# Three products of 256 columns made into one of 512 and one of 256, in a float32 expert layer split into high and low parts

## The chip, the core and the metric

The kernel runs on one core of a Trainium2 chip. The metric is the device time of one execution in microseconds, median of several runs. The engines are TensorE (PE: matrix products; PEld: its weight loads), VectorE (DVE), ScalarE (ACT), GpSimd (POOL) and SyncE (SP, which issues all transfers of weights). Each runs its own list of instructions in order; semaphores tie the lists together.

## The reference

Three blocks work on 256 tokens of 1024 features: two layers of mixer and expert feed-forward, then one attention and pooling block. The change touches only the expert layers, which take most of the time:

```python
def peer_ffn(x, norm_ffn, w_query, sub_keys, expert_down, expert_up):   # twice
    xn = rmsnorm(x, norm_ffn)
    q = (xn @ w_query).reshape(B, S, 8, 2, 128)       # w_query 1024 x 2048
    s = einsum('bthpd,hpnd->bthpn', q, sub_keys)      # 128 keys, two halves, 8 heads
    s1, i1 = top_k(s[..., 0, :], 16); s2, i2 = top_k(s[..., 1, :], 16)
    top_s, top_c = top_k(all sums s1 + s2, 16)
    idx = i1[top_c // 16] * 128 + i2[top_c % 16]
    g = softmax(top_s)
    act = gelu(einsum('btd,bthkd->bthk', xn, expert_down[idx]))
    return einsum('bthk,bthkd->btd', g * act, expert_up[idx])  # 16384 experts
```

## The kernel before

Instead of gathering experts, the kernel computes all 16384 for all tokens, and multiplies by a gate that is zero where an expert was not picked. Each float32 operand is split in two parts of the type fp32r: high (a copy) and low (the difference). A product is the sum of high·high, high·low and low·high: three matrix products (`three`, lines 170 to 173), each with a weight load of its own.

Weights stream in chunks of 128 x 1024 values (512 KB), in four slots. For each chunk SP loads `raw` (`load`), ACT writes the high part `WH` (`high`, L154) once PE has left the slot, DVE (`low_v`, L159) or POOL (`low_g`, L164) writes the low part `WL`, and PE uses both. `on_gpsimd` names the chunks whose low part POOL makes: all of the queries ("wq"), and "down" chunks 0 to 31.

An expert layer has, per layer, 16 chunks of queries, 128 of "down" and 128 of "up". The functions `peer_tensor`, `peer_scalar` and `peer_vector` write the order of PE, ACT and DVE by hand, one step of the loop per chunk c:

- Queries: chunks 2h and 2h+1 fill two PSUM banks with head h, 256 tokens wide. ACT copies them to `QT` (L991). PE multiplies by the keys (`key_scores`, L861) one chunk later, ACT copies the scores (L942), and DVE picks the best 16 (`top16`, L1031 to L1039).
- Selection: after the last head DVE runs `select_pairs` (L1057 to L1102), one chain of some 60 us. PE turns the picks (`turn_picked`, L870, which waits for the semaphore `picked`) behind down chunk 28, and DVE makes tables of them (`picked_tables`, L1115 to L1126).
- Down: the weights are the expert chunk (stationary), the tokens XH and XL move, 256 columns at a time; a chunk takes 8 k-steps of `three` = 24 products. Two chunks share a bank, and ACT applies gelu from the bank to the array `G` (L1014).
- Gates: from chunk 29 on (SPREAD), 8 tokens every 3 chunks (PACE), 32 groups: DVE writes one-hot tables (L1136, L1142, L1147), ACT scales rows (L952, 8 per group), PE multiplies them (`products`, L882, 16 small products) into one of two pairs of banks, and DVE folds the gates into what `G` holds so far (L1154), ACT copies them ahead for the experts still to come (L958). For tokens whose gates are already there, gelu stays in PSUM (L1016) and DVE multiplies (L1164).
- Up: `G` is split in parts (L974, L1169) and is the weight operand; the expert chunk moves, 512 columns at a time, 12 products per chunk.

Of the kernel before, what the change touches and what calls it, by code (L numbers as in the profile page):

```python
# [7 lines left out]
ALU = mybir.AluOpType  # L8
# [9 lines left out]
NW = 4  # L18
# [53 lines left out]
def build(nc, d, out):  # L72
    ctx = ExitStack()
    with ctx:
# [7 lines left out]
        XH = sb("XH", [128, 8, 256], F32R)  # L82
        XL = sb("XL", [128, 8, 256], F32R)
# [15 lines left out]
        sb("ONE_REST", [128, 2048])  # L99
        CST = sb("cst", [128, C_N0])  # L100
# [701 lines left out]
        keys_in, wq_up, key_mm, s_up = (sem(n) for n in ("keys_in", "queries_up", "key_products", "key_scores"))  # L802
        arg_up, arg_exp, tk_up, tk_T, it_up = (sem(n) for n in (
# [5 lines left out]
        SPREAD, PACE, GROUPS = 29, 3, 32  # L809

        def fold_chunk(s):
            return SPREAD + PACE * s + 4

        def open_tokens(c):
            return 8 * sum(fold_chunk(s) <= c for s in range(GROUPS))


        TAILS, HEADS = {-1: 0}, {-1: 0}
# [3 lines left out]
        N_TAIL, N_HEAD = TAILS[127], HEADS[127]  # L822
# [3 lines left out]
        def parts_g(p):  # L826
            if p % 3 == 0:
                return GH, GL_
            return [v[:, 2 * (p % 3):2 * (p % 3) + 2, :].rearrange("p e t -> p (e t)") for v in (XH, XL)]
# [5 lines left out]
        def gate_bank(s):  # L835
            return 4 + 2 * (s % 2)

        def gate_view(s):

            b = gate_bank(s)  # L840
            return PS[:, b:b + 2, :].rearrange("p a n -> p (a n)").rearrange("p (t i) -> p i t", t=8)
# [10 lines left out]
        def key_scores(t, l, h):  # L852
            if h == 0:
                t.wait_ge(keys_in, 16 * l + 16)
            t.wait_ge(wq_up, 16 * l + 2 * h + 2)
# [17 lines left out]
        def products(t, l, s):  # L873
            t.wait_ge(col_s, 32 * l + s + 1)
            t.wait_ge(row_0, 256 * l + 8 * s + 8)
            t.wait_ge(row_1, 32 * l + s + 1)
            if s >= 2:
                t.wait_ge(fold_a, 32 * l + s - 1)
            for j in range(8):
                g, tt = divmod(j, 2)  # L880
                for k in range(2):
                    m = t.matmul(PS[:, gate_bank(s) + j // 4, (j % 4) * 128:(j % 4) * 128 + 128],  # L882
                                 ONE[:, s % 2, 0, g, :, tt], ROWS[:, s % 2, 1 + k, g, :, tt], start=(k == 0), stop=(k == 1))
            m.then_inc(prod, 1)

        def peer_tensor(t, l):
            wq, down, up = bases(l)
            n = 2 * l + 1
            norm_tensor(t, n, XS)

            def q_bank(pair, j):
                if pair >= 2:
                    t.wait_ge(wq_up, 16 * l + 2 * pair - 3 + j)
            for c in range(16):
                pair, kh = divmod(c, 2)
                chunk_T(t, wq + c, [PS[:, 2 * (pair % 2) + j, 0:256] for j in range(2)], 0, kh, 8,
                        n if pair == 0 else None, lambda j: q_bank(pair, j))
                if c >= 2 and c % 2 == 0:
                    key_scores(t, l, c // 2 - 1)
            for c in range(128):  # L900
                wait_low(t, down + c)
                if c < 8 and c % 2 == 0:
                    t.wait_ge(wq_up, 16 * l + 13 + c // 2)
                if c % 2 == 0 and c >= 8:
                    if open_tokens(c - 7):
                        t.wait_ge(act_gated, N_HEAD * l + HEADS[c - 7])
                    else:
                        t.wait_ge(act_tail, N_TAIL * l + TAILS[c - 7])
                o = PS[:, (c // 2) % 4, (c % 2) * 256:(c % 2) * 256 + 256]
                for k in range(8):  # L910
                    m = three(t, o, [v[:, (down + c) % NW, k * 128:k * 128 + 128] for v in (WH, WL)],
                              [v[:, k, :] for v in (XH, XL)], k == 0, k == 7)
                m.then_inc(w_used, 1)
                if c == 0:
                    key_scores(t, l, 7)
                if c == SPREAD - 1:
                    turn_picked(t, l)
                s, r = divmod(c - SPREAD - 3, PACE)
                if r == 0 and 0 <= s < GROUPS:
                    products(t, l, s)  # L920
            for c in range(128):
                p, j = divmod(c, 2)
                i = up + c
                wait_low(t, i)
                if j == 0:
                    t.wait_ge(g_low, 64 * l + p + 1)
                    if c == 0:
                        t.wait_ge(fold_a, 32 * l + 32)
                gh, gl = parts_g(p)
# [24 lines left out]

        def fold_scalar(a, l, s, c):
            n = c - c % 2
            a.wait_ge(fold_v, 32 * l + s + 1)
            a.activation(G[:, n:128, 8 * s:8 * s + 8], gate_view(s)[:, n:128], ACT.Copy).then_inc(fold_a, 1)  # L958
# [17 lines left out]
        def peer_scalar(a, l):  # L976
# [4 lines left out]
            for c in range(16):  # L981
# [3 lines left out]
                if c % 2:  # L985
# [4 lines left out]
                    for j in range(2):  # L990
                        a.activation(QT[:, 2 * pair + j, :], PS[:, 2 * (pair % 2) + j, 0:256], ACT.Copy).then_inc(wq_up, 1)  # L991
            for c in range(128):
# [3 lines left out]
                if c == SPREAD - 14:  # L996
                    gate_exp(a, l)
                s, r = divmod(c - SPREAD - 1, PACE)
# [4 lines left out]
                s, r = divmod(c - SPREAD - 4, PACE)  # L1003
                if r == 0 and 0 <= s < GROUPS:
                    fold_scalar(a, l, s, c)
                if c == 127:
                    split_g_scalar(a, l, 0)
                if c % 2:
                    ps, g, k = pair_view((c // 2) % 4), G[:, c - 1:c + 1, :], open_tokens(c)
                    a.wait_ge(w_used, down + c + 1)  # L1010
                    if c == 77:
                        a.wait_ge(it_up, l + 1)
                    if k < 256:
                        a.activation(g[:, :, k:256], ps[:, :, k:256], ACT.Gelu_apprx_tanh).then_inc(act_tail, 1)  # L1014
                    if k:
                        a.activation(ps[:, :, 0:k], ps[:, :, 0:k], ACT.Gelu_apprx_tanh).then_inc(act_head, 1)  # L1016
# [23 lines left out]

        def select_keys(v, l):
            for h in range(8):
                v.wait_ge(s_up, 8 * l + h + 1)
# [105 lines left out]
        def fold_vector(v, l, s, c):  # L1149
            n = c - c % 2  # L1150
# [3 lines left out]
            v.tensor_tensor(g, gate_view(s)[:, 0:n], g, ALU.mult).then_inc(fold_v, 1)  # L1154

        def gate_vector(v, l, c):

            k = open_tokens(c)
# [5 lines left out]
            v.tensor_tensor(g, pair_view((c // 2) % 4)[:, :, 0:k], g, ALU.mult).then_inc(act_gated, 1)  # L1164
# [17 lines left out]
        def peer_vector(v, l):  # L1182
# [10 lines left out]
            for c in range(128):  # L1193
                low_v(v, down + c + 2)
                if c % 2 == 0 and c > 0:
                    gate_vector(v, l, c - 1)
                s, r = divmod(c - SPREAD, PACE)
                if 0 <= s < GROUPS:
                    (onehots, scale_columns, rows_part1)[r](v, l, s)
                s, r = divmod(c - SPREAD - 4, PACE)  # L1200
                if r == 0 and 0 <= s < GROUPS:
                    fold_vector(v, l, s, c)
                if c == 127:
                    split_g_vector(v, l, 0)
            gate_vector(v, l, 127)
# [1130 lines left out]
```

## Time and profile before

| | |
|---|---|
| median of 3 runs | 2197.97 us (2196.89 to 2198.56) |
| profiled execution | 2198.79 us; its span 2197.0 us, mean granted clock 0.994 |
| PE, PEld busy | 98%, 90% |
| DVE, ACT, POOL busy | 63%, 56%, 17% |
| HBM read | 369.96 MB, 169 GB/s over the span |

In the first layer queries run from 146 to 197 us, down from 197 to 598 us, up from 598 to 946 us; the second layer has the same stages, some 937 us later. Busy shares are of the whole span. A PE record of a product is longer than the distance to the next one, as products overlap, so what a product costs is read from start to start.

### The profile page before, as it was taken

What the parts mean: (1) busy time and instruction counts of PE and PEld (TensorE: products, weight loads), DVE (VectorE), ACT (ScalarE), POOL (GpSimd) and SP (SyncE); (2) the same over time, 40 slices, a digit from 0 to 9 for tenths busy, and PEclk for the clock granted to TensorE, in tenths of its full rate; (3) what the DMA queues carried; (4) which work ended last, traced back from release to release, by engine and by line L of the source; (5) the groups of instructions that cost most, each with busy time, mean ns of one, the idle gap of its engine ahead of it and who ended that gap; (6) DMA issues with size and microseconds to landing.
All of it is one profiled execution on the core that took longest, in us unless ns stands there. A gap on an engine that the chain in (4) does not pass through costs nothing.

```text
span 2197.0 us, 36208 instructions
## 1 busy us (share of the span) xinstructions
PE 2154.4 (98%) x14640; PEld 1968.7 (90%) x14640; DVE 1378.2 (63%) x2369; ACT 1235.9 (56%) x2086; POOL 370.3 (17%) x168
## 2 busy tenths in 40 slices
PE   8899999999999999997999999999999999999998
PEld 7789999999988888876899999999888888898997
DVE  7657867777755555557479567777555555423445
ACT  6654567777644444465555677776444444444463
POOL 1437810000000000001378100000000000243131
PEclk9999999999999999999999999999999999999999
DMA  6444554455566666642345545544666666754233
GB/s 217 145 135 164 184 172 164 163 164 167 162 200 192 195 196 191 192 161 94 125 161 186 173 160 168 167 162 163 201 192 192 192 194 194 250 188 145 84 130 115
DMA packets 104330, 373.41 MB, mean 170 GB/s; under 512 B 11565, under 2 KB 15045, under 8 KB 103781
## 3 DMA queue, kind: packets, MB, share of 16 engines
q1 hardware_dynamic: 104164, 371.11, 52.3%
q8 instruction: 116, 1.90, 0.3%
q14 instruction: 50, 0.40, 0.1%
HBM read 369.96 MB, written 1.10 MB: 169 GB/s over the span
## 4 chain that ended last, share of the span: by engine, by line
PE 92%; DVE 3%; ACT 2%; DMA 1%; issue 1%; POOL 0%; SPq 0%; ACTq 0%; DVEq 0%
PE ps L171 28%; PE ps L172 28%; PE ps L173 28%; PE ps L882 3%; PE ps L1862 1%; PE ps L1840 1%; DMA raw<-in_w_qk_dram 1%; DVE WL L159 1%; PE ps L267 1%; PE ps L861 1%; PE ps L1848 0%; DVE arena L1598 0%; PE ps L277 0%; PE ps L1322 0%; ACT WH L154 0%
## 5 line engine op out<-in xcount | busy, mean ns | idle before, releaser
L154 ACT ACTIVATE WH<-raw 128x1024 fp32r<-128x1024 f32 x680 | 717.5, 1057 | 541.4 <-PE ps L173 525.3
L171 PE MATMUL ps<-XH,WH 128*128 128x256 f32 x2816 | 807.3, 287 | 3.7 <-DVE XL L2146 2.8
L172 PE MATMUL ps<-XL,WH 128*128 128x256 f32 x2816 | 797.7, 283 | 0.0
L173 PE MATMUL ps<-XH,WL 128*128 128x256 f32 x2816 | 797.5, 283 | 0.0
L159 DVE TENSOR_TENSOR WL<-raw,WH 128x1024 fp32r<-128x1024 f32 x548 | 670.5, 1226 | 102.9 <-ACT WH L154 102.5
L171 PEld LDWEIGHTS ps<-XH,WH 128*128 128x128 f32 x2816 | 540.9, 192 | 9.4 <-DVE XL L2146 3.0
L172 PEld LDWEIGHTS ps<-XL,WH 128*128 128x128 f32 x2816 | 541.5, 192 | 0.1
L173 PEld LDWEIGHTS ps<-XH,WL 128*128 128x128 f32 x2816 | 541.0, 192 | 0.0
L164 POOL TENSOR_TENSOR WL<-raw,WH 128x1024 fp32r<-128x1024 f32 x132 | 328.6, 2494 | 1011.1 <-ACT WH L154 1010.2
L171 PE MATMUL ps<-WH,XH 128*128 128x512 f32 x960 | 379.1, 395 | 4.4 <-DVE XL L725 1.6
L172 PE MATMUL ps<-WL,XH 128*128 128x512 f32 x960 | 375.8, 391 | 0.0
L173 PE MATMUL ps<-WH,XL 128*128 128x512 f32 x960 | 375.7, 391 | 0.0
L171 PEld LDWEIGHTS ps<-WH,XH 128*128 128x128 f32 x960 | 181.6, 189 | 45.1 <-issue 2.0
L173 PEld LDWEIGHTS ps<-WH,XL 128*128 128x128 f32 x960 | 181.5, 189 | 38.3
L172 PEld LDWEIGHTS ps<-WL,XH 128*128 128x128 f32 x960 | 181.4, 189 | 37.5 <-issue 0.5
L952 ACT ACTIVATE ONE<-ONE,GATE 128x128 f16<-128x128 f16 x512 | 167.3, 428 | 0.0
L1169 DVE TENSOR_TENSOR XL<-arena,XH 128x512 fp32r<-128x512 f32 x84 | 58.1, 692 | 164.9 <-ACT XH L974 164.9
L1014 ACT ACTIVATE arena<-ps 128x512 f32<-128x512 f32 (+31 forms) x126 | 55.3, 439 | 147.6 <-PE ps L173 147.5
L171 PE MATMUL ps<-WH,GH 128*128 128x512 f32 x352 | 137.0, 389 | 0.0
L172 PE MATMUL ps<-WL,GH 128*128 128x512 f32 x352 | 137.0, 389 | 0.0
L173 PE MATMUL ps<-WH,GL 128*128 128x512 f32 x352 | 136.9, 389 | 0.0
L1758 POOL TENSOR_TENSOR arena<-arena,trig 128x128 f32<-128x128 f32 x8 | 4.2, 555 | 722.0 <-DVE arena L1598 722.0
(279 smaller groups left out, 1829.5 us busy)
## 6 DMA issues: line engine op xcount, KB each, us to landing
raw<-in_l_down_dram SPq DMA_DIRECT2D x256, 512.0 KB, 3.4
raw<-in_l_up_dram SPq DMA_DIRECT2D x256, 512.0 KB, 3.9
raw<-in_l_wq_dram SPq DMA_DIRECT2D x32, 512.0 KB, 3.4
raw<-in_w_qk_dram SPq DMA_DIRECT2D x24, 512.0 KB, 3.5
raw<-in_w_gates_dram SPq DMA_DIRECT2D x24, 512.0 KB, 3.5
raw<-in_l_nat_dram SPq DMA_DIRECT2D x16, 512.0 KB, 3.9
raw<-in_l_wout_dram SPq DMA_DIRECT2D x16, 512.0 KB, 3.5
raw<-in_l_win_dram SPq DMA_DIRECT2D x16, 512.0 KB, 4.1
```

Of the source, the lines that this page charges most:

```text
L154: a.activation(WH[:, i % NW, :], raw[:, i % NW, :], ACT.Copy).then_inc(w_high, 1)
L159: v.tensor_tensor(WL[:, i % NW, :], raw[:, i % NW, :], WH[:, i % NW, :], ALU.subtract).then_inc(w_low_v, 1)
L164: g.tensor_tensor(WL[:, i % NW, :], raw[:, i % NW, :], WH[:, i % NW, :], ALU.subtract).then_inc(w_low_g, 1)
L171: t.matmul(o, a[0], b[0], start=first, stop=False)
L172: t.matmul(o, a[0], b[1], start=False, stop=False)
L173: return t.matmul(o, a[1], b[0], start=False, stop=last)
L267: t.matmul(PS[:, bank, 384:512], ident, ident, start=True, stop=True)
L861: m = t.matmul(PS[:, 4 + h % 4, (2 * tt + q) * 128:(2 * tt + q) * 128 + 128], QT[:, j, tt * 128:tt * 128 + 128], KEYS[:, j * 128:j * 128 + ...
L882: m = t.matmul(PS[:, gate_bank(s) + j // 4, (j % 4) * 128:(j % 4) * 128 + 128], ONE[:, s % 2, 0, g, :, tt], ROWS[:, s % 2, 1 + k, g, :, tt ...
L952: a.activation(ROWS[:, s % 2, 1, g, :, t], ROWS[:, s % 2, 2, g, :, t], ACT.Copy, scale=GATE0[:, 8 * s + j:8 * s + j + 1]).then_inc(row_0, 1)
L1014: a.activation(g[:, :, k:256], ps[:, :, k:256], ACT.Gelu_apprx_tanh).then_inc(act_tail, 1)
L1169: v.tensor_tensor(gl, G[:, 2 * p:2 * p + 2, :].rearrange("p e t -> p (e t)"), gh, ALU.subtract).then_inc(g_low, 1)
```

## The change

- XH and XL lie side by side for each k in one tile X2 (128 x 8 x 2 x 256). `two` multiplies the high weights by both at once (512 columns, a whole bank), then the low weights by XH (256 columns, into the bank's lower half). It replaces `three` in the 16 query chunks and in down chunks 26 to 127 (WIDE = 26) of each layer. The halves of a bank have to be added afterwards.
- Queries: ACT copies the upper halves (128x512 for two banks, `queries_low`), DVE adds the lower ones (`queries`, new, 8 per layer); the add for head h+1 stands before `top16` of head h.
- Down from 26 on: each chunk has a bank of its own, six in turn (0 to 5). For each pair ACT copies the upper halves to BESIDE (`copy_beside`), DVE adds (`down_add`: tokens without gates into `G`, the others into PSUM), and ACT applies gelu one loop step later (`gelus`). `products` now has only banks 6 and 7.
- Gates are spread from chunk 25 on: `turn_picked` stands behind down chunk 24 and chunk 26 waits for the tables (`it_up`). `rows_part1` and the fold stand a chunk later against the group's first step, `gate_vector` and the copies of `fold_scalar` too.
- POOL makes the low parts of down chunks 0 to 27 only.

```diff
-        return name[3:] == "wq" or c < 32
+        return name[3:] == "wq" or c < 28
-        XH = sb("XH", [128, 8, 256], F32R)
-        XL = sb("XL", [128, 8, 256], F32R)
+        X2 = sb("X2", [128, 8, 2, 256], F32R)
+        XH, XL = X2[:, :, 0, :], X2[:, :, 1, :]
+        def two(t, bank, w, k, first, last):
+            t.matmul(PS[:, bank, :], w[0], X2[:, k, :, :].rearrange("p w t -> p (w t)"), start=first, stop=False)
+            return t.matmul(PS[:, bank, 0:256], w[1], X2[:, k, 0, :], start=False, stop=last)
...
-        SPREAD, PACE, GROUPS = 29, 3, 32
+        SPREAD, PACE, GROUPS = 25, 3, 32
+        WIDE = 26
-            return SPREAD + PACE * s + 4
+            return SPREAD + PACE * s + 5
+        def down_bank(c):
+            return (c - WIDE + 4) % 6 if c >= WIDE else (c // 2) % 4
...
# products
-            if s >= 2:
-                t.wait_ge(fold_a, 32 * l + s - 1)
+            if s >= 1:
+                t.wait_ge(fold_a, 32 * l + s)
# peer_tensor, down
+                before = bank_before(c) if c % 2 == 0 else None
+                if c == WIDE:
+                    t.wait_ge(it_up, l + 1)
+                elif before is not None:
...
+                    if c >= WIDE:
+                        m = two(t, b, w, k, k == 0, k == 7)
+                    else:
+                        m = three(...)
                 if c == SPREAD - 1:
                     turn_picked(t, l)
-                s, r = divmod(c - SPREAD - 3, PACE)
+                s, r = divmod(c - SPREAD - 4, PACE)
# ACT, new
+        def copy_beside(a, l, c):
+            n, b = pair_at(c), down_bank(c - 1)
+            a.wait_ge(w_used, bases(l)[1] + c + 1)
+            if c - 4 > WIDE:
+                a.wait_ge(added, N_ADD * l + ADDS[c - 4])
+            a.activation(BESIDE[:, n % 2], PS[:, b:b + 2, 256:512], ACT.Copy).then_inc(beside, 1)
# DVE, new
+        def queries(v, l, h):
+            q = QT[:, 2 * h:2 * h + 2, :]
+            v.wait_ge(wq_low, 8 * l + h + 1)
+            v.tensor_tensor(q, PS[:, 2 * (h % 2):2 * (h % 2) + 2, 0:256], q, ALU.add).then_inc(wq_up, 1)
+        def down_add(v, l, c):
+            k, n, b = open_tokens(c), pair_at(c), down_bank(c - 1)
+            v.wait_ge(beside, PAIRS * l + n + 1)
+            if k < 256:
+                v.tensor_tensor(G[:, c - 1:c + 1, k:256], PS[:, b:b + 2, k:256], BESIDE[:, n % 2, :, k:256],
+                                ALU.add).then_inc(added, 1)
+            if k:
+                o = PS[:, b:b + 2, 0:k]
+                v.tensor_tensor(o, o, BESIDE[:, n % 2, :, 0:k], ALU.add).then_inc(added, 1)
# peer_vector, down loop
-                if c % 2 == 0 and c > 0:
-                    gate_vector(v, l, c - 1)
+                if c % 2 == 0 and c > WIDE:
+                    down_add(v, l, c - 1)
                 s, r = divmod(c - SPREAD, PACE)
-                if 0 <= s < GROUPS:
-                    (onehots, scale_columns, rows_part1)[r](v, l, s)
+                if r == 0 and 1 <= s <= GROUPS:
+                    rows_part1(v, l, s - 1)
+                if r == 0 and 0 <= s < GROUPS:
+                    onehots(v, l, s)
+                if r == 1 and 0 <= s < GROUPS:
+                    scale_columns(v, l, s)
...
+                if c % 2 and c > WIDE + 1:
+                    gate_vector(v, l, c - 2)
```

PE behind down chunk 24, first the program before (there 24 is like any other chunk; its picks come behind 28), then the changed one at the turning of the picks. L171 to L173 are `three`, L870 is `turn_picked`:

```order
L173 MATMUL ps<-XH,WL 128x256
L171 MATMUL ps<-XH,WH 128x256
L172 MATMUL ps<-XL,WH 128x256
L173 MATMUL ps<-XH,WL 128x256
L870 MATMUL ps<-cst,arena 128x128 [waits key_scores,picked]
```

After the change L172 to L174 are `three`, L891 is `turn_picked`, and L178 and L179, from chunk 26 on, are `two`:

```order
L174 MATMUL ps<-X,WL 128x256
L891 MATMUL ps<-cst,arena 128x128 [waits key_scores,picked]
L891 MATMUL ps<-cst,arena 128x128 x5
L172 MATMUL ps<-X,WH 128x256 [waits w_low_g]
...
L178 MATMUL ps<-X,WH 128x512
L179 MATMUL ps<-X,WL 128x256
L178 MATMUL ps<-X,WH 128x512
L179 MATMUL ps<-X,WL 128x256
```

The picks are turned with one full chunk (25) between them and the first `two`.

DVE in the down stage, some three chunks of the program before, in the middle of the gates' spreading (L159 low part, L1164 gate, L1147 `rows_part1`, L1136 one-hots, L1142 scaling, L1154 fold):

```order
L159 TENSOR_TENSOR WL<-raw,WH 128x1024 [waits w_high]
L1164 TENSOR_TENSOR arena<-ps,arena 128x2x88 [waits gates_copied,gelu_open]
L1147 TENSOR_TENSOR ONE<-ONE,GP 128x1024 [waits rows_part0]
L159 TENSOR_TENSOR WL<-raw,WH 128x1024 [waits w_high]
L1136 TENSOR_TENSOR ONE<-IOT,IB 128x1024 [waits gate_products]
L1136 TENSOR_TENSOR ONE<-IOT,IB 128x1024
L159 TENSOR_TENSOR WL<-raw,WH 128x1024 [waits w_high]
L1164 TENSOR_TENSOR arena<-ps,arena 128x2x88 [waits gates_copied,gelu_open]
L1142 TENSOR_TENSOR ONE<-ONE,EB 128x1024 [waits onehots]
L1154 TENSOR_TENSOR arena<-ps,arena 128x66x8 [waits gelu_new,gate_products]
```

The same place after (L160 low part, L1229 and L1233 `down_add`, L1215 `rows_part1`, L1204 one-hots, L1210 scaling, L1243 gate, L1222 fold):

```order
L160 TENSOR_TENSOR WL<-raw,WH 128x1024 [waits w_high]
L1229 TENSOR_TENSOR arena<-ps,BESIDE 128x2x192 [waits down_beside]
L1233 TENSOR_TENSOR ps<-ps,BESIDE 128x2x64
L1215 TENSOR_TENSOR ONE<-ONE,GP 128x1024 [waits rows_part0]
L1204 TENSOR_TENSOR ONE<-IOT,IB 128x1024 [waits gate_products]
L1204 TENSOR_TENSOR ONE<-IOT,IB 128x1024
L160 TENSOR_TENSOR WL<-raw,WH 128x1024 [waits w_high]
L1210 TENSOR_TENSOR ONE<-ONE,EB 128x1024 [waits onehots]
L1243 TENSOR_TENSOR arena<-ps,arena 128x2x64 [waits gates_copied,gelu_open]
L160 TENSOR_TENSOR WL<-raw,WH 128x1024 [waits w_high]
L1229 TENSOR_TENSOR arena<-ps,BESIDE 128x2x184 [waits down_beside]
L1233 TENSOR_TENSOR ps<-ps,BESIDE 128x2x72
```

Two adds per pair of chunks are new, and `rows_part1` has moved to stand directly before the next group's one-hots.

## Rows read from the trace of the kernel before

**Rows 1.** Windows: selection, early and late gates, up (busy us; clock; DMA).

```profile
core 0: us, PE busy (x) PEld busy (x) DVE busy (x) ACT busy (x) POOL busy (x), PEclk, DMA share, GB/s
200.33:281.00 80.67, 80.67 (x675) 80.67 (x674) 66.18 (x182) 41.25 (x47) 68.04 (x29) 1.00 0.55 181
300.00:396.13 96.13, 96.13 (x882) 95.70 (x882) 66.70 (x95) 69.84 (x151) 0.00 (x0) 1.00 0.50 165
492.00:588.13 96.13, 96.13 (x883) 95.70 (x882) 76.69 (x95) 67.50 (x152) 0.00 (x0) 1.00 0.51 163
600.00:930.00 330.00, 330.00 (x1457) 273.26 (x1456) 186.63 (x184) 159.65 (x182) 0.00 (x0) 1.00 0.62 194
```

**Rows 2.** The page's chain that ended last, its line by engine.

```profile
PE 92%; DVE 3%; ACT 2%; DMA 1%; issue 1%; POOL 0%; SPq 0%; ACTq 0%; DVEq 0%
```

**Rows 3.** Timeline of PE, products of 256 columns: down chunks 1 to 28.

```profile
200.53 0.28 PE L172 MATMUL ps<-XL,WH 128*128 128x256 f32 x1
...
280.93 0.28 PE L173 MATMUL ps<-XH,WL 128*128 128x256 f32 x1
281.05 0.82 PE L870 MATMUL ps<-cst,arena 128*128 128x128 f32 x6
281.62 0.36 PE L171 MATMUL ps<-XH,WH 128*128 128x256 f32 x1
```

**Rows 4.** Timeline of PE, products of 512 columns at the end of up.

```profile
937.98 0.39 PE L171 MATMUL ps<-WH,XH 128*128 128x512 f32 x1
...
945.91 0.39 PE L173 MATMUL ps<-WH,GL 128*128 128x512 f32 x1
```

**Rows 5.** The critical chain, first and last gate products (start, us).

```profile
293.37 0.93 PE ps L882 x16
...
591.38 0.94 PE ps L882 x16
```

**Rows 6.** DVE timeline, late gates (start, us, idle before).

```profile
586.35 0.67 DVE L1164 TENSOR_TENSOR arena<-ps,arena 128x496 f32<-128x496 f32 x1 [0.40 <-ACT ps L1016]
588.53 0.69 DVE L1147 TENSOR_TENSOR ONE<-ONE,GP 128x1024 f16<-128x1024 f16 x1 [1.50 <-ACT ONE L952]
```

**Rows 7.** Waits of DVE in 492 to 588 us (us, times, longest).

```profile
DVE ONE L1147 <- ACT ONE L952: 16.8, 10, 1.9
DVE arena L1164 <- ACT ps L1016: 2.8, 5, 0.7
```

**Rows 8.** Adds of PSUM and SBUF while POOL works: DVE, then POOL.

```profile
136.37 0.69 DVE L232 TENSOR_TENSOR X<-X,ps 128x512 f32<-128x512 f32 x1 [0.67 <-PE ps L173]
136.21 2.39 POOL L164 TENSOR_TENSOR WL<-raw,WH 128x1024 fp32r<-128x1024 f32 x1 [0.32 <-ACT WH L154]
```

**Rows 9.** ACT copies of 128x512 from PSUM, end of queries.

```profile
200.62 0.60 ACT L942 ACTIVATE arena<-ps 128x512 f32<-128x512 f32 x1 [2.17 <-PE ps L861]
```

**Rows 10.** DVE in the selection: last heads, pairs, picks, tables.

```profile
194.60 0.87 DVE L1031 MAX8 arena<-arena 128x8 f32<-128x128 f32 x4 [1.87 <-ACT arena L942]
199.09 0.28 DVE L1034 FIND_INDEX8 arena<-arena 128x8 uint32<-128x128 f32 x1
201.25 0.87 DVE L1031 MAX8 arena<-arena 128x8 f32<-128x128 f32 x4 [1.87 <-ACT arena L942]
229.23 3.93 DVE L1068 TENSOR_TENSOR arena<-arena 128x128 f32<-128x128 f32 x2
234.18 2.38 DVE L1078 TENSOR_SCALAR arena<-arena 128x256 uint32<-128x256 uint32 x1
267.01 0.90 DVE L1102 TENSOR_TENSOR arena<-arena,sm 128x128 f32<-128x128 f32 x2
281.90 0.76 DVE L1115 CAST IB<-ps 128x256 bf16<-128x256 f32 x2 [13.99 <-PE ps L870]
284.21 0.42 DVE L1126 TENSOR_TENSOR GP<-arena,GATE 128x256 f16<-128x256 f32 x1
```

**Rows 11.** POOL in the selection, low parts of the down chunks.

```profile
233.91 4.91 POOL L164 TENSOR_TENSOR WL<-raw,WH 128x1024 fp32r<-128x1024 f32 x2 [0.91 <-ACT WH L154]
```

More of the change, by code:

```diff
@@ L99, in build @@
         sb("ONE_REST", [128, 2048])
+        BESIDE = sb("BESIDE", [128, 2, 2, 256])
         CST = sb("cst", [128, C_N0])
@@ L808, in build @@
         g_high, g_low = sem("act_high"), sem("act_low")
-        SPREAD, PACE, GROUPS = 29, 3, 32
+        SPREAD, PACE, GROUPS = 25, 3, 32
+        WIDE = 26
+        beside, added = sem("down_beside"), sem("down_added")
         def fold_chunk(s):
-            return SPREAD + PACE * s + 4
+            return SPREAD + PACE * s + 5
         def open_tokens(c):
-            return 8 * sum(fold_chunk(s) <= c for s in range(GROUPS))
-        TAILS, HEADS = {-1: 0}, {-1: 0}
+            return 8 * sum(fold_chunk(s) <= c + 1 for s in range(GROUPS))
+        TAILS, HEADS, ADDS = {-1: 0}, {-1: 0}, {WIDE - 1: 0}
         for c in range(1, 128, 2):
@@ L821, in build, with bank_before, pair_at @@
             HEADS[c] = HEADS[c - 2] + (open_tokens(c) > 0)
-        N_TAIL, N_HEAD = TAILS[127], HEADS[127]
+            if c > WIDE:
+                ADDS[c] = ADDS[c - 2] + (open_tokens(c) < 256) + (open_tokens(c) > 0)
+        N_TAIL, N_HEAD, N_ADD = TAILS[127], HEADS[127], ADDS[127]
+        PAIRS = (128 - WIDE) // 2
+        GATE_EXP = 15
+        def down_bank(c):
+            return (c - WIDE + 4) % 6 if c >= WIDE else (c // 2) % 4
+        def bank_before(c):
+            mine = {down_bank(c), down_bank(c + 1)}
+            return max((b for b in range(1, c, 2) if mine & {down_bank(b - 1), down_bank(b)}), default=None)
+        def pair_at(c):
+            return (c - WIDE) // 2
         ROWS, GP16, EXP2 = ONE[:, :, :, :, :, :].bitcast(F16), GP.bitcast(F16), EB[:, :]
@@ L828, in parts_g @@
                 return GH, GL_
-            return [v[:, 2 * (p % 3):2 * (p % 3) + 2, :].rearrange("p e t -> p (e t)") for v in (XH, XL)]
+            return [X2[:, 2 * (p % 3) + i, :, :].rearrange("p w t -> p (w t)") for i in range(2)]
         def bases(l):
@@ L889, in peer_tensor @@
             norm_tensor(t, n, XS)
-            def q_bank(pair, j):
-                if pair >= 2:
-                    t.wait_ge(wq_up, 16 * l + 2 * pair - 3 + j)
             for c in range(16):
                 pair, kh = divmod(c, 2)
-                chunk_T(t, wq + c, [PS[:, 2 * (pair % 2) + j, 0:256] for j in range(2)], 0, kh, 8,
-                        n if pair == 0 else None, lambda j: q_bank(pair, j))
+                wait_low(t, wq + c)
+                if kh == 0 and pair >= 2:
+                    t.wait_ge(wq_up, 8 * l + pair - 1)
+                for j in range(2):
+                    for kk in range(4):
+                        k = kh * 4 + kk
+                        if pair == 0 and j == 0:
+                            wait_x(t, n, k)
+                        m = two(t, 2 * (pair % 2) + j, [v[:, (wq + c) % NW, kk * 256 + j * 128:kk * 256 + j * 128 + 128]
+                                                        for v in (WH, WL)], k, k == 0, k == 7)
+                m.then_inc(w_used, 1)
                 if c >= 2 and c % 2 == 0:
@@ L902, in peer_tensor @@
                 if c < 8 and c % 2 == 0:
[L903 to L906, printed above, removed]
-                    else:
-                        t.wait_ge(act_tail, N_TAIL * l + TAILS[c - 7])
-                o = PS[:, (c // 2) % 4, (c % 2) * 256:(c % 2) * 256 + 256]
+                    t.wait_ge(wq_up, 8 * l + 7 + c // 4)
+                before = bank_before(c) if c % 2 == 0 else None
+                if c == WIDE:
+                    t.wait_ge(it_up, l + 1)
+                elif before is not None:
+                    if open_tokens(before):
+                        t.wait_ge(act_gated, N_HEAD * l + HEADS[before])
+                    else:
+                        t.wait_ge(act_tail, N_TAIL * l + TAILS[before])
+                b = down_bank(c)
                 for k in range(8):
-                    m = three(t, o, [v[:, (down + c) % NW, k * 128:k * 128 + 128] for v in (WH, WL)],
-                              [v[:, k, :] for v in (XH, XL)], k == 0, k == 7)
+                    w = [v[:, (down + c) % NW, k * 128:k * 128 + 128] for v in (WH, WL)]
+                    if c >= WIDE:
+                        m = two(t, b, w, k, k == 0, k == 7)
+                    else:
+                        m = three(t, PS[:, b, (c % 2) * 256:(c % 2) * 256 + 256], w, [v[:, k, :] for v in (XH, XL)],
+                                  k == 0, k == 7)
                 m.then_inc(w_used, 1)
@@ L953, in rows_scalar, with fold_from, gelus @@
                              scale=GATE0[:, 8 * s + j:8 * s + j + 1]).then_inc(row_0, 1)
+        def fold_from(c):
+            return c - 1 if c % 2 else c - 2
         def fold_scalar(a, l, s, c):
-            n = c - c % 2
+            n = fold_from(c)
             a.wait_ge(fold_v, 32 * l + s + 1)
-            a.activation(G[:, n:128, 8 * s:8 * s + 8], gate_view(s)[:, n:128], ACT.Copy).then_inc(fold_a, 1)
+            a.activation(G[:, n:128, 8 * s:8 * s + 8], gate_view()[:, n:128], ACT.Copy).then_inc(fold_a, 1)
+        def copy_beside(a, l, c):
[4 more added lines that the diff above has]
+            a.activation(BESIDE[:, n % 2], PS[:, b:b + 2, 256:512], ACT.Copy).then_inc(beside, 1)
+        def gelus(a, l, c):
+            k, g = open_tokens(c), G[:, c - 1:c + 1, :]
+            b, n = down_bank(c - 1), N_ADD * l + ADDS[c - 2]
+            if k < 256:
+                n += 1
+                a.wait_ge(added, n)
+                a.activation(g[:, :, k:256], g[:, :, k:256], ACT.Gelu_apprx_tanh).then_inc(act_tail, 1)
+            if k:
+                o = PS[:, b:b + 2, 0:k]
+                a.wait_ge(added, n + 1)
+                a.activation(o, o, ACT.Gelu_apprx_tanh).then_inc(act_head, 1)
         def split_g_scalar(a, l, p):
@@ L989, in peer_scalar @@
                     a.wait_ge(w_used, wq + c + 1)
-                    for j in range(2):
-                        a.activation(QT[:, 2 * pair + j, :], PS[:, 2 * (pair % 2) + j, 0:256], ACT.Copy).then_inc(wq_up, 1)
+                    a.activation(QT[:, 2 * pair:2 * pair + 2, :], PS[:, 2 * (pair % 2):2 * (pair % 2) + 2, 256:512],
+                                 ACT.Copy).then_inc(wq_low, 1)
             for c in range(128):
@@ L995, in peer_scalar @@
                 high(a, down + c + 3)
-                if c == SPREAD - 14:
+                if c == GATE_EXP:
                     gate_exp(a, l)
+                s, r = divmod(c - 1 - fold_chunk(0), PACE)
+                if r == 0 and 0 <= s < GROUPS:
+                    fold_scalar(a, l, s, c - 1)
                 s, r = divmod(c - SPREAD - 1, PACE)
@@ L1002, in peer_scalar @@
                     rows_scalar(a, l, s, range(4 * r, 4 * r + 4))
-                s, r = divmod(c - SPREAD - 4, PACE)
-                if r == 0 and 0 <= s < GROUPS:
-                    fold_scalar(a, l, s, c)
+                if c > WIDE and c % 2 == 0:
+                    gelus(a, l, c - 1)
                 if c == 127:
                     split_g_scalar(a, l, 0)
-                if c % 2:
-                    ps, g, k = pair_view((c // 2) % 4), G[:, c - 1:c + 1, :], open_tokens(c)
+                if c % 2 and c < WIDE:
                     a.wait_ge(w_used, down + c + 1)
[L1011 to L1016, printed above, removed]
+                    a.activation(G[:, c - 1:c + 1, :], pair_view(down_bank(c)), ACT.Gelu_apprx_tanh).then_inc(act_tail, 1)
+                elif c % 2:
+                    copy_beside(a, l, c)
+            gelus(a, l, 127)
             for c in range(128):
```

31 lines of the change are left out of this document (19 added, 12 removed).

## The prediction, made before the changed kernel ran

> **What bounds the kernel now.** I read the table of busy time by stage first. In the selection, in the early and late gates and in up, PE is busy for the whole of every window, at the full granted clock, while DVE, the next one, is busy 66.70 of 96.13 us early and 76.69 of 96.13 us late [rows 1]. The chain that ended last says the same of the whole program: 92% of it is PE [rows 2]. So in the stages that change, time is the number of products times their distance, as long as nobody makes PE wait.
>
> The distances come from the timeline of PE. From the start at 200.53 to that at 280.93 lie 670 steps of 256 columns: 80.40 / 670 = 0.1200 us [rows 3]. From 937.98 to 945.91 lie 35 steps of 512 columns: 7.93 / 35 = 0.2266 us [rows 4]. The difference, 0.1066 us, is 256 columns at 2.4 GHz; so a product costs its columns (0.1067 or 0.2133 us) and about 0.0133 us more, whatever its width. The gate products come every (591.38 - 293.37) / 31 = 9.613 us [rows 5]: three down chunks of 24 x 0.1200 = 2.88 us, and 0.97 us for the products themselves and the change of kind.
>
> **PE, the gain.** A k-step was 3 x 0.1200 = 0.3600 us. It becomes one product of 512 and one of 256 columns: 0.2266 + 0.1200 = 0.3466 us. The columns are the same 768; one fixed part of 0.0134 us goes. Per layer 16 query chunks and 102 down chunks change, 8 k-steps each: 2 x 118 x 8 = 1888 products fewer, and 1888 x 0.0134 = 25.3 us. No row shows the two widths in turn. Bounds: if the narrow product hid behind the wide one's load to its bare columns, a step would be 0.2266 + 0.1067 and the gain 50 us; if the weight load that now follows a narrow product had to be shown in full, a step would stay at 0.36 and the gain be nothing. I take 25.3, as both rows have the same fixed part though the loads are under a 256-column product in one and a 512-column product in the other.
>
> The Trainium skill, "TensorE: Matmul & The Clock Gate", section "Back-to-back issue gap", gives the warm gap as columns / 2.4 plus 2.5 ns. By that estimate the removed fixed part is worth 1888 x 2.5 ns = 4.7 us. The rows disagree with it: both widths have 13.3 ns.
>
> **DVE, the cost that must be hidden.** Down from 26 on adds, per pair of chunks, an add of 128x512 from PSUM and SBUF, usually cut in two. The nearest row takes 0.69 us [rows 8], of which about 0.60 us counts start to start; with some 0.07 us for the cut, 1.5 pairs per period of three chunks cost 1.5 x 0.67 = 1.0 us. A period of PE shrinks to 9.613 - 3 x 8 x 0.0134 = 9.29 us. DVE's work late in the stage is now 76.69 / 10 = 7.67 us per period [rows 1] and becomes 8.7 us, 93% of 9.29; early it is 6.67 + 1.0 = 7.7. It fits, but only if DVE hardly waits: 0.6 us are free late.
>
> At present DVE waits there (16.8 + 2.8) / 10 = 1.96 us per period, 1.7 of it for ACT's scaled rows [rows 7], which `rows_part1` wants right behind the one-hots [rows 6]. The new order puts it a chunk (2.8 us) later, while ACT's part stays in place; the longest such wait is 1.9 us, so it goes. The wait for gelu (0.4 us) goes likewise, as the gate now stands a chunk later. New waits of DVE: `down_add` for `copy_beside`, ready one ACT copy (bound 0.60 us, [rows 9]) after PE has left the pair; behind it are queued this step's tables and the next low part. That low part, of chunk c+3 when the pair c-2, c-1 is added, is wanted by PE some three chunks (8.3 us) later, and before it stand at most the add (0.7), tables (1.9) and one more low part (1.2): 4 us to spare. `fold_vector` waits for `products`, 0.97 us after a chunk's end; laid out over six chunks (18.6 us) late in the stage, with this wait and the adds, DVE still comes round about 1 us early. So PE doesn't see it: cost 0, and if the cover is gone, what DVE has over 9.29 us per period, up to 64 times.
>
> ACT adds 1.5 x 0.5 = 0.75 us per period to 67.50 / 10 = 6.75 us (late; early 6.98) [rows 1]: 7.7 of 9.29 us at most, hidden. The bank that PE waits for has six chunks between two uses; add, gelu and gate need about two. `products` with one pair of banks waits for the copy of the last fold, which stands more than a chunk ahead. SP issues the same transfers; DMA is busy 0.51 here and 0.62 in up, where a chunk lasts 2.72 us [rows 1], less than the new 2.77. POOL drops four low parts per layer to DVE, which has just started the gates then: hidden.
>
> **The queries.** DVE gets 8 adds. A head takes PE 2 x 2.77 + 0.9 = 6.45 us, and DVE's `top16` 199.37 - 194.60 = 4.8 us [rows 10] plus the add, 0.6: it fits. But `top16` of head 6 now stands behind the add for head 7, so it starts 1.2 us after the last query chunk instead of 2.2 us before it. Worked through: the last query chunk ends at 196.8 - 1.7 = 195.1 (16 x 8 x 0.0134 = 1.7 earlier), copy and add end at 196.3, head 6 at 201.1, head 7 at 205.9, where it was 206.0. So the chain of the selection begins at the same time, and 1.6 us later against PE.
>
> **The picks, where PE may wait.** The chain ends at 267.91 [rows 10]; PE turned the picks at 281.05 [rows 3], and DVE had waited 13.99 us. Now they are turned four chunks sooner, 4 x 2.88 = 11.5, and PE is 1.7 ahead: about 267.8. So of 13 us of cover nothing is left, and PE waits between 0 and a little over 2 us. What decides is POOL: DVE's operations with both inputs in SBUF stretch while POOL runs: two subtractions of 128x128 took 3.93 us, and one of 128x256, started just before POOL's next pair, 2.38 us [rows 10, 11]. DVE thus goes on in POOL's gaps, and POOL moves with PE, 1.7 us earlier. If the chain keeps its gap it ends at 266.2, and PE doesn't wait; if it misses one it ends one POOL operation (2.4 us) later, 268.6, and PE waits 0.9. I take 0.2 as the mean.
>
> The Trainium skill, "SBUF — State Buffer", section "Who interferes with whom", says that a DVE instruction with both inputs in SBUF and a reading GpSimd instruction exclude each other for the whole instruction. The trace agrees with the 3.93 us. It also clears the new adds, which read one input from PSUM, as the 0.69 us beside a running POOL does [rows 8].
>
> Then `it_up`: from the turning's start to the end of the tables are 284.6 - 281.0 = 3.6 us [rows 10, 3]; PE has the turning (0.6) and chunk 25 (2.9, still three products) in between: it waits about 0.2 us. Together 0.4 us per layer, 0.8 in all; bounds 0 and 6 us for both layers.
>
> **Sum.** -25.3 + 0.8 = -24.5 us. Against the profiled execution, 2198.79 us (its span 2197.0 and 1.8 around it), that is 2174.3; the median of the runs is 0.8 lower, so 2197.97 - 24.5 = 2173.5 us.
>
> **Rivals.**
> - *PE waits a little in many places* (picks that miss POOL's gaps in both layers, DVE late in the last third of each down stage). For: 93% is no comfortable share. Price: 2 x 2 us for the picks and 0.2 us in some 20 periods: 2177 to 2183.
> - *DVE's waits stay and DVE becomes the bound; the slower side.* Place: the gate periods. If the 1.96 us of waits per period are not slack but latency between the engines, a period takes 9.61 + 1.0 = 10.6 us instead of 9.29, over 64 periods +64 us against before, less some 5 us gained in the queries and outside the gates: about 2257. It decides against the change from 9.61 - 8.7 = 0.9 us of waits kept per period. Against: the order moves away just what it waits for, and DVE works one to three chunks ahead of PE's need.
> - *The fixed part isn't given back, or only some of it.* If a wide and a narrow product in turn take 0.36 us: 2198, no change. The gate products show that a fixed part can be smaller: 16 of 128 columns take 0.94 us [rows 5], 0.0588 each, 0.0054 over their columns. If a removed product gives back only as much, the gain is 1888 x 0.0054 = 10 us, and the time 2189. Against: those are 16-bit products, while both rows of fp32r have 13.3 ns. The skill's gap, weighed above, would put this case at 2194.
> - *The change overshoots:* the narrow product costs its bare columns, 2173.5 - 25 = 2149. No row speaks for it.
>
> **How the numbers follow.** Forecast 74% (own range 2172 to 2177), small waits 13%, DVE the bound 4%, fixed part kept 5% (3% no change, 2% at 2189), overshoot 2%, other waits between 2183 and 2193 2%. Less than 0.2% (4.4 us) can't be told from no change. Range 2171 to 2182: it takes the forecast and most of the small waits, some 84%. Faster 92%, same 4%, slower 4%.
>
> **What would show it.** In the gates' stage the distance between gate products: 9.29 us if right; a wide product every 0.347 us. DVE's busy share there 93% late, its waits for L952 gone, and no idle time of PE but for a few tenths at the turned picks and at chunk 26. Wrong: a distance above 9.4 us, PE waiting for low parts or gated banks, or a k-step that isn't 0.347 us.

## The result

| | before | changed |
|---|---|---|
| median of 4 runs | 2198.26 us (2196.89 to 2199.42) | 2179.40 us (2176.28 to 2179.70) |
| profiled execution | 2198.79 us, span 2197.0 | 2179.14 us, span 2177.4 |

The ratio is 0.9912, 95% interval 0.9899 to 0.9924: 18.9 us less. The forecast was 2173.5 (range 2171 to 2182): right in sign and kind. The time is 5.9 us above it, and the gain of 18.9 us is 5.6 us short of the 24.5 forecast.

The profile after. The table of busy time by stage, early and late gates, and up (as [rows 1]):

```profile
core 0: us, PE busy (x) PEld busy (x) DVE busy (x) ACT busy (x) POOL busy (x), PEclk, DMA share, GB/s
300.00:394.00 94.00, 94.00 (x642) 82.00 (x641) 77.46 (x126) 77.09 (x166) 0.00 (x0) 1.00 0.55 168
478.00:572.00 94.00, 94.00 (x643) 82.00 (x642) 85.32 (x124) 73.28 (x166) 0.00 (x0) 1.00 0.55 168
590.00:930.00 340.00, 340.00 (x1502) 281.51 (x1501) 191.69 (x190) 167.23 (x193) 0.00 (x0) 1.00 0.62 193
```

PE is still busy throughout; DVE has gone from 80% to 91% of the late window. Its waits in 480 to 574 us (as [rows 7]; columns are us in all, times, longest):

```profile
DVE arena L1229 <- ACT BESIDE L1005: 4.7, 7, 1.0
DVE arena L1222 <- PE ps L903: 3.2, 5, 0.6
DVE arena L1243 <- ACT arena L997: 0.6, 1, 0.6
DVE WL L160 <- ACT WH L155: 0.2, 1, 0.2
```

The 16.8 us of waits for ACT's scaled rows are gone, and the waits foreseen in their place (`down_add` for the copy, the fold for the gate products) are there, 0.9 us per group in all. The picks and the tables, timeline of PE (as [rows 3]):

```profile
268.28 0.82 PE L891 MATMUL ps<-cst,arena 128*128 128x128 f32 x6
268.86 0.36 PE L172 MATMUL ps<-X,WH 128*128 128x256 f32 x1
...
271.68 0.28 PE L174 MATMUL ps<-X,WL 128*128 128x256 f32 x1
272.02 0.47 PE L178 MATMUL ps<-X,WH 128*128 128x512 f32 x1
```

and DVE there (as [rows 10]):

```profile
266.02 0.65 DVE L1170 TENSOR_TENSOR arena<-arena,sm 128x128 f32<-128x128 f32 x2
269.14 0.75 DVE L1183 CAST IB<-ps 128x256 bf16<-128x256 f32 x2 [2.47 <-PE ps L891]
```

The picks end at 266.67, 1.6 us before PE turns them (13.99 us of DVE's waiting became 2.47), and for the tables PE waits 0.34 - 0.12 = 0.22 us. All that as forecast. What was not: the distance of the gate products, in the critical chain (as [rows 5]; start, us):

```profile
283.36 0.93 PE ps L903 x16
292.83 0.94 PE ps L903 x16
302.14 0.94 PE ps L903 x16
311.61 0.94 PE ps L903 x16
...
574.53 0.94 PE ps L903 x16
```

The distance is 9.47 and 9.31 in turn, (574.53 - 283.36) / 31 = 9.393 on average, not 9.29. PE never idles there; its k-steps differ. From a long stretch (first) and from the short one behind it, starts of wide (L178) and narrow (L179) products:

```profile
472.34 0.40 PE L178 MATMUL ps<-X,WH 128*128 128x512 f32 x1
472.57 0.28 PE L179 MATMUL ps<-X,WL 128*128 128x256 f32 x1
472.69 0.40 PE L178 MATMUL ps<-X,WH 128*128 128x512 f32 x1
472.93 0.28 PE L179 MATMUL ps<-X,WL 128*128 128x256 f32 x1
473.05 0.40 PE L178 MATMUL ps<-X,WH 128*128 128x512 f32 x1
...
473.40 0.40 PE L178 MATMUL ps<-X,WH 128*128 128x512 f32 x1
...
481.80 0.40 PE L178 MATMUL ps<-X,WH 128*128 128x512 f32 x1
...
482.49 0.40 PE L178 MATMUL ps<-X,WH 128*128 128x512 f32 x1
...
483.54 0.39 PE L178 MATMUL ps<-X,WH 128*128 128x512 f32 x1
```

473.40 - 472.34 = 1.06 us for three steps, 0.3533 each; 483.54 - 481.80 = 1.74 for five, 0.348, and 0.3467 over the whole stretch behind its first, longer step. The rate holds from one block of small products (gates or keys) to the next. Taken over the trace, 848 of the 1888 k-steps lie in long stretches: 16 of the 31 between groups in each layer, and 40 k-steps of each layer's queries. 848 x 0.0066 = 5.6 us.

### The profile page after: what moved, and what is told of

Its sections match the earlier page's. It is cut to its first block, busy times and chain, and to the rows that moved or that the text cites. A ratio compares the mean times of both kernels' runs of the same rounds, so it can differ in the third digit from the quotient of the medians.

```text
span 2177.4 us, 32842 instructions
## 1 busy us (share of the span) xinstructions
PE 2133.0 (98%) x12752; PEld 1857.8 (85%) x12752; DVE 1464.9 (67%) x2593; ACT 1278.1 (59%) x2172; POOL 349.4 (16%) x160
## 4 chain that ended last, share of the span: by engine, by line
PE 91%; DVE 4%; ACT 2%; DMA 1%; issue 1%; POOL 0%; SPq 0%; ACTq 0%; DVEq 0%
PE ps L178 20%; PE ps L172 18%; PE ps L174 17%; PE ps L173 17%; PE ps L179 10%; PE ps L903 3%; PE ps L1948 1%; DVE WL L160 1%; PE ps L1926 1%; DMA raw<-in_w_qk_dram 1%; PE ps L273 1%; PE ps L882 1%; PE ps L1934 0%; DVE arena L1684 0%; ACT WH L155 0%
## 5 line engine op out<-in xcount | busy, mean ns | idle before, releaser
L160 DVE TENSOR_TENSOR WL<-raw,WH 128x1024 fp32r<-128x1024 f32 x556 | 679.7, 1224 | 105.8 <-ACT WH L155 105.8
L178 PE MATMUL ps<-X,WH 128*128 128x512 f32 x1888 | 670.8, 399 | 0.1
L179 PE MATMUL ps<-X,WL 128*128 128x256 f32 x1888 | 526.9, 279 | 0.0
L178 PEld LDWEIGHTS ps<-X,WH 128*128 128x128 f32 x1888 | 354.3, 188 | 81.3 <-issue 0.5
L172 PE MATMUL ps<-WH,X 128*128 128x512 f32 x960 | 379.0, 395 | 4.6 <-DVE X L731 1.6
L173 PE MATMUL ps<-WL,X 128*128 128x512 f32 x960 | 374.9, 391 | 0.0
L174 PE MATMUL ps<-WH,X 128*128 128x512 f32 x960 | 374.8, 390 | 0.0
L179 PEld LDWEIGHTS ps<-X,WL 128*128 128x128 f32 x1888 | 356.0, 189 | 0.0
L172 PE MATMUL ps<-X,WH 128*128 128x256 f32 x928 | 265.4, 286 | 3.8 <-DVE X L2232 2.8
L173 PE MATMUL ps<-X,WH 128*128 128x256 f32 x928 | 262.6, 283 | 0.0
L174 PE MATMUL ps<-X,WL 128*128 128x256 f32 x928 | 262.6, 283 | 0.0
L172 PEld LDWEIGHTS ps<-WH,X 128*128 128x128 f32 x960 | 181.2, 189 | 45.4 <-issue 2.0
L174 PEld LDWEIGHTS ps<-WH,X 128*128 128x128 f32 x960 | 181.0, 189 | 38.4
L173 PEld LDWEIGHTS ps<-WL,X 128*128 128x128 f32 x960 | 181.3, 189 | 37.1 <-issue 0.5
L172 PEld LDWEIGHTS ps<-X,WH 128*128 128x128 f32 x928 | 177.9, 192 | 9.6 <-DVE X L2232 3.0
L173 PEld LDWEIGHTS ps<-X,WH 128*128 128x128 f32 x928 | 178.0, 192 | 0.1
L174 PEld LDWEIGHTS ps<-X,WL 128*128 128x128 f32 x928 | 178.0, 192 | 0.0
L1248 DVE TENSOR_TENSOR X<-arena,X 128x512 fp32r<-128x512 f32 x84 | 58.1, 692 | 161.9 <-ACT X L1034 161.9
L172 PE MATMUL ps<-WH,GH 128*128 128x512 f32 x352 | 137.0, 389 | 0.0
```

The costliest lines, as they stand in the source:

```text
L160: v.tensor_tensor(WL[:, i % NW, :], raw[:, i % NW, :], WH[:, i % NW, :], ALU.subtract).then_inc(w_low_v, 1)
L178: t.matmul(PS[:, bank, :], w[0], X2[:, k, :, :].rearrange("p w t -> p (w t)"), start=first, stop=False)
L179: return t.matmul(PS[:, bank, 0:256], w[1], X2[:, k, 0, :], start=False, stop=last)
L1248: v.tensor_tensor(gl, G[:, 2 * p:2 * p + 2, :].rearrange("p e t -> p (e t)"), gh, ALU.subtract).then_inc(g_low, 1)
```

## The experiments

Theory A: a wide and a narrow product in turn have two rates, and the state in which PE comes back from the small products decides which. Theory B: the new copies and adds on the same banks disturb PE in some stretches. Each kernel's `before` median on its chip is given; the gate distances are from its own trace. One kernel's runs lie up to 5 us apart, so the theories, which differ by a few us, are judged by the distances, and the medians only go beside them.

**Products of one width.** For k over 0 (k = 0 keeps its wide product):

```diff
-            t.matmul(PS[:, bank, :], w[0], X2[:, k, :, :]...)
+            for half in range(2):
+                t.matmul(PS[:, bank, 256 * half:256 * half + 256], w[0], X2[:, k, half, :], ...)
```

> The changed kernel, but for k over 0 the wide product is again two of 256 columns (into the two halves of the bank): 1652 products more, all copies, adds and orders as changed. It separates the width from everything else. Theory A (two step rates): a k-step of a wide and a narrow product takes 0.3467 us in some stretches and 0.3533 in others, by the state in which PE enters the stretch, and costs 5.6 us; with products of one width a k-step is 0.3600 everywhere, gate products are 9.60 us apart without alternation, and the time is 2179.4 + 848 x 7/8 x 0.0067 + 804 x 0.0133 + ... = about 2196. Theory B (copies and adds on the banks disturb PE's writes): the alternation stays, with k-steps of 0.360 and some 0.367, gate products 9.6 and 9.77 us apart, about 2201.

Measured: 2198.8 us (2197.42 before), ratio 1.0002 (0.9993 to 1.0011). The chain:

```profile
284.85 0.93 PE ps L907 x16
294.44 0.94 PE ps L907 x16
304.02 0.94 PE ps L907 x16
```

9.59 us everywhere, no alternation, with all copies and adds in place: B falls, and the new work of DVE and ACT costs PE nothing (the kernel before has 9.61). Nearly the whole gain hangs on the width. The time is 2.8 us above what A gave. In the profiled execution the last block, which the change doesn't touch, took 316.3 us, against 313.7 in the kernel before and 311.0 in the changed one; PE stands 2.4 us longer there before its first product of streamed weights than in either. Up to that block this kernel is 1.4 us faster than the one before.

**Widths grouped.**

```diff
-                for k in range(8): wide(k); narrow(k)
+                for k in range(8): wide(k)
+                for k in range(8): narrow(k)
```

> The changed kernel with the same products in another order: all wide ones of a chunk (of four k in the queries), then all narrow ones. Theory A: the rows of one width in a row are constant, so a chunk takes 8 x (0.2267 + 0.1200) = 2.773 us in every stretch, gate products 9.30 us apart without alternation, about 2179.4 - 5.6 = 2174. Theory B: the same adds and copies meet the same banks, every other distance stays 0.16 us longer, 2179.

Measured: 2180.02 us (2197.42), ratio 0.9921 (0.9907 to 0.9934). In the chain a chunk reads

```profile
285.56 1.90 PE ps L949 x8
287.46 0.95 PE ps L950 x8
288.41 1.84 PE ps L949 x8
290.25 0.95 PE ps L950 x8
...
293.99 0.94 PE ps L903 x16
```

The groups are evenly 9.37 us apart. So the alternation goes with the strict change of widths, as A says. But A had 9.30 and 2174, and both failed: eight wide products take 1.84 where 8 x 0.2267 = 1.81, so a change of width costs something however rarely it comes. The time is near what B gave, but without B's alternation.

**Narrow first at odd k.** (`if k % 2: narrow(k); wide(k)`)

> The changed kernel with the narrow product ahead of the wide one at odd k: wide, narrow, narrow, wide, and so on. Theory A: the alternation of widths is cut down to every second place; if the slow rate needs the strict alternation, no slow stretches, 2174; if it comes from each change of width, half of the cost stays, 2176 to 2177. Theory B: as before, 2179.

Measured: 2178.89 us (2197.42), ratio 0.9916 (0.9902 to 0.9929); groups evenly 9.36 us apart. No alternation, and a distance between the two; neither of A's times (2174, or 2176 to 2177) was met; 2179 was B's time, but B falls with the alternation.

**Narrow first at k = 7 alone.**

> The changed kernel with the narrow product ahead of the wide one at k = 7 alone, so each chunk ends in a wide product and the next begins with one. Theory A: PE enters and leaves the gate products in another order of widths; if that decides the state, the stretches are all alike, at best 9.30 us per group, 2174; at worst all at 9.47, 2184. Theory B: alternation as in the changed kernel, 2179.

Measured: 2177.89 us (2197.64), ratio 0.9911 (0.9898 to 0.9925); groups evenly 9.37 us apart, neither of the two ends that were expected (9.30 or 9.47). This 9.37 isn't a third rate. The timeline of PE, wide products of one stretch, in its first and in its third chunk:

```profile
377.70 0.40 PE L179 MATMUL ps<-X,WH 128*128 128x512 f32 x1
...
378.74 0.39 PE L179 MATMUL ps<-X,WH 128*128 128x512 f32 x1
...
382.57 0.40 PE L179 MATMUL ps<-X,WH 128*128 128x512 f32 x1
...
383.63 0.40 PE L179 MATMUL ps<-X,WH 128*128 128x512 f32 x1
```

Three steps take 1.04 us in the first chunk and 1.06 in the third: the short rate and the long one, in one stretch, with no small product in between. The three chunks take 2.86 (with the longer first step), 2.79 and 2.82 us in each of the 62 stretches between groups. So a swapped pair, too, changes the rate; A, which let only the entry into the stretch decide, is too narrow.

**One more gate product.** In `products`, for the last j:

```diff
+                for _ in range(1 if j == 7 else 0):
+                    t.matmul(PS[:, 7, 384:512], ..., start=True, stop=True)
```

> The changed kernel with a 17th gate product per group (the last product is made once more ahead of itself, its result is overwritten): 64 x 0.0586 = 3.75 us more work. Theory A: the state in which PE leaves the group changes, so another set of stretches is slow: all fast 2177.5, all slow 2189, the same share 2183. Theory B: adds and copies are the same, the same every other stretch is slow, 2183.

Measured: 2178.79 us (2197.42), ratio 0.9915 (0.9900 to 0.9930). The chain has the groups at

```profile
283.38 0.82 PE ps L906 x14
292.75 0.82 PE ps L906 x14
302.12 0.82 PE ps L906 x14
```

9.37 us: 9.31 and the extra product, in both layers. Nothing between two blocks was touched, and the long stretches are gone. This is the clearest sign for A: the block has a say in how the stretch behind it runs.

**Two more.** (`range(2 ...)`)

> Two repeated gate products per group, 18 in all, 7.5 us more work. If the state is kept or toggled by the number of products between two stretches (16 toggles, 17 doesn't), 18 toggles again, with groups 9.43 and 9.59 us apart, 2187; if any addition to the block keeps PE fast, all are 9.43 us apart, 2182.

Measured: 2187.85 us, one run (2197.64). The time is near the first forecast, the distances are neither:

```profile
283.57 0.82 PE ps L906 x14
292.99 0.82 PE ps L906 x14
302.42 0.82 PE ps L906 x14
312.00 0.82 PE ps L906 x14
321.43 0.82 PE ps L906 x14
```

9.43, 9.43, 9.58: every third stretch is long. So it isn't a switch that odd and even numbers flip, but something that comes round after three.

**One more, short.** (16 columns instead of 128)

> The 17th gate product has 16 columns instead of 128. If the number of products sets the state, all stretches are fast as with a long one, groups 9.35 to 9.37 us apart, 2178; if the time at which PE comes back sets it, the alternation or an all-slow state can return, 9.51 us, 2187.

Measured: 2179.27 us, one run (2197.64); all groups 9.34 us apart.

**The changed kernel again.**

> The changed kernel unaltered, beside the variants on one chip: 2179.4 us, gate products alternately 9.31 and 9.47 us apart (theories A and B alike).

Measured: 2178.66 us (2176.41 to 2180.84; before 2197.64), ratio 0.9913 (0.9899 to 0.9927). The first layer alternates. The second, with the same instructions:

```profile
1213.11 0.94 PE ps L903 x16
1222.43 0.93 PE ps L903 x16
1231.74 0.93 PE ps L903 x16
1241.05 0.93 PE ps L903 x16
```

9.31 us throughout. So the program alone doesn't fix the state: within a layer it never changes its pattern, between two layers of one execution it does. It is then set at or before the first group; by what, these runs don't show. A layer without long stretches is 2.3 us shorter (from first to last group 291.0 and 288.7 us). The changed kernel's runs lie 3 to 5 us apart, but that is no sign of it: the runs of the kernel before lie 2.4 to 4.5 apart, and those with products of one width 5.2.

**Row tables early**, the slower rival put to the test (the edit in effect, not word for word):

```diff
-                if r == 0 and 1 <= s <= GROUPS:
-                    rows_part1(v, l, s - 1)
+                if r == 2 and 0 <= s < GROUPS:
+                    rows_part1(v, l, s)
```

> The changed kernel with rows_part1 back where the program before has it, a chunk earlier, where DVE has to wait for ACT's scaled rows (1.7 us per group in the program before). The prediction's slower rival: waits come back and DVE, at 93% of a period, falls behind; PE waits for low parts or banks, groups over 9.5 us apart, 2185 to 2250. If DVE has room even with such waits, because it gives them back elsewhere: groups 9.39 us apart, 2179.

Measured: 2178.77 us (2198.59), ratio 0.9909 (0.9893 to 0.9926). DVE's waits in 480 to 574 us:

```profile
DVE ONE L1215 <- ACT ONE L987: 7.6, 8, 1.5
DVE arena L1222 <- PE ps L903: 0.9, 1, 0.9
```

The wait is back and takes the place of the others, 8.5 us in all against 8.7. PE doesn't wait; this time the first layer has only short stretches (9.31) and the second alternates. DVE's waits are slack: moved, not added.

**Gates from chunk 24 on.** (`SPREAD = 24`)

> The changed kernel with the gates spread from chunk 24 on, so the picks are turned one chunk (2.88 us) earlier and two chunks lie between them and the first wide product. In the changed kernel's trace DVE had the picks ready 1.8 us before PE turned them. So PE waits about 1.1 us at the turning in each layer, and not at all (0.2 less) for the tables: about 2 us more in all, 2181, but for a change of the slow stretches (up to 5.6 us either way).

Measured: 2182.3 us (2198.59), ratio 0.9926 (0.9910 to 0.9943). The timeline of PE at the turning:

```profile
266.73 0.87 PE L891 MATMUL ps<-cst,arena 128*128 128x128 f32 x6 [1.14 <-DVE arena L1170]
```

1.14 us, in both layers, as expected; both alternate, so the long stretches don't hide it. One chunk sooner is past the picks' cover.

**The short product, timed**, beside the changed kernel once more:

> The kernel with one repeated gate product of 16 columns per group again, now timed, as its groups were 9.34 us apart throughout the first layer. Theory A with the state set by the phase at which PE comes back: both layers fast again, 62 x (9.39 - 9.34) = 3 us less than the changed kernel where that alternates in both layers: 2176. If the phase at entry differs from run to run, it alternates in some runs and the medians are equal, 2178 to 2179.

> The changed kernel beside it on the same chip: 2178.5 to 2179.5, some runs 2.3 us lower where one layer doesn't alternate.

Measured on one chip: 2176.98 us (2175.89 to 2178.03) and 2180.61 (2177.89 to 2183.01), before 2198.46; ratios 0.9903 (0.9888 to 0.9918) and 0.9919 (0.9906 to 0.9933). With the short product both layers are even:

```profile
282.63 0.82 PE ps L906 x14
291.97 0.82 PE ps L906 x14
301.31 0.82 PE ps L906 x14
```

In the changed kernel both alternate. In the two traces a product that computes nothing new makes the gates of a layer 1.6 us shorter (289.5 against 291.2 us from first to last group), 3.3 us in all; against two layers that happen to be short (288.7 each) it would cost 1.6. The medians differ by 3.6 us, but the two intervals overlap, and on the earlier chip the one run of this kernel (2179.27) was no faster than the changed kernel (2178.66): that it makes the kernel faster as a rule isn't shown.

## Why the prediction was right, and where it was off

- **What bounds the kernel:** right. PE's distances make the time; with products of one width (but for k = 0) in the changed kernel's frame the time is that of the kernel before.
- **PE's gain:** the step that was off. "I take 25.3, as both rows have the same fixed part" holds in the short stretches (0.3467 us per k-step, forecast 0.3466). In 848 of 1888 steps it was 0.3533, so the term is 25.3 - 5.6 = 19.7 us. The prediction said that no row shows the two widths in turn, and gave the step two bounds, but took one value for all stretches. Its own sign of being wrong, a distance above 9.4 us, stands in every second stretch; only the mean, 9.39, stays below. The estimate from the Trainium skill, "TensorE: Matmul & The Clock Gate", section "Back-to-back issue gap", whose formula is for a product by itself, would have given 4.7 us; the measured gain speaks for the 13.3 ns of the rows.
- **Luck:** 2179.4 lies within the range, but outside the forecast's own range (2172 to 2177). It lies where the rival of small waits was put (2177 to 2183), and those waits made 0.4 us. That the missing 5.6 us fell inside a width allowed for another cause is luck.
- **DVE:** right in mechanism and size: 85.32 / 94.00 = 91% late (forecast 93%), old waits gone, no wait of PE. The slower rival fell twice: with the old order of the row tables DVE waits for ACT again (7.6 us in ten periods, where it was 16.8), and PE still doesn't wait.
- **Picks:** forecast a chain end of 266.2 or 268.6 against a turning at 267.8; measured 266.67 against 268.28. The chain kept its gap of POOL: POOL's next operation begins at 267.23, 1.24 us earlier than before, and the chain's end moved by the same 1.24 us, not by 1.7. Waits 0 and 0.22 us per layer, 0.4 in all where 0.8 was forecast. Of the cover 1.6 us was left, less than a chunk, as the step to chunk 24 shows.
- **Copies, banks, transfers:** hidden, as forecast.
- **Sum:** 25.3 - 5.6 - 0.4 = 19.3 us, against 18.9 by the medians and 19.65 by the profiled executions. The remainder is of the size that stages the change doesn't touch differ by between executions: the last block, from its first idle products to the end, took 313.70 us in the profile before and 311.02 in the one after, which flatters the latter by 2.7 us; in the changed layers alone the two profiles differ by 17.7 us. Of the 1.6 us that this is below 19.3, about 1.1 lie in the gates: a short distance is 9.31 us rather than 9.29.

The prediction misread one row. It counted L1078, 2.38 us, among DVE's operations "with both inputs in SBUF", but the row is a TENSOR_SCALAR, which reads one tensor. The same form takes 0.28 us in POOL's gap, in the kernel before:

```profile
233.08 0.28 DVE L1071 TENSOR_SCALAR arena<-arena 128x256 uint32<-128x256 uint32 x1
```

So, to judge by these two rows, an operation of one tensor can stretch beside POOL as well. The forecast of the chain's end doesn't depend on it.

Open: what it is that PE carries across the small products. The runs show that it changes with the length of the block and with a swapped pair inside a stretch, not what hardware keeps it, nor what sets it at a layer's first group. Whether the changed kernel's fastest runs had one even layer or two can't be told, as only profiled executions show it.

## What to carry to other kernels

Where PE bounds, merging products that share weights saves the fixed part of each product removed, and can be counted from two start-to-start distances; but take the distance in the very mix that the new code issues, or keep a second value for it. Before moving a consumer ahead, subtract all that shifts on either side from the wait that covers it: here 13.99 us shrank to 2.5, and one chunk more would have cost 1.1 us per layer. And read the distance between repeated markers one by one: a mean of 9.39 us hid 9.31 and 9.47.

## What the runs showed of the hardware that was not expected

- A wide (512) and a narrow (256) fp32r product in strict turn take 0.3467 or 0.3533 us per pair, the same rate from one block of 16-bit or key products to the next. Long rows of one width have 0.120 or 0.227 in the expert layers.
- The sequence of rates depends on the block between: with 16 small products alternating (eight of the ten layers profiled) or all short (two); with 17 all short in the six layers profiled (9.37 us per group with the long extra product, 9.34 with the short); with 18 every third long. In the queries, where the block is the key products, one stretch of three is long.
- The same program shows either sequence in its two layers in one execution.
- Changing the order inside the pair, or grouping the widths, gives groups evenly 9.36 and 9.37 us apart. With one swapped pair per chunk this is made of chunks at the short and at the long rate in one stretch.
